# Moving two thirds of a conditioning product from TensorE to VectorE, and loading expert weights in 2 MiB pieces, in a hybrid attention and mixture-of-experts layer

## The reference, cut to what matters

```python
mod = c @ w_ada + b_ada                       # (1, 6144): six vectors of 1024
sh1, sc1, g1, sh2, sc2, g2 = split(mod, 6)
h = rms_norm(x, norm1_g) * (1 + sc1) + sh1    # x: 256 tokens x 1024
proj = h @ w_in                               # 8192 columns
merged = sigmoid(ga) * (diff_attention @ w_pa) + sigmoid(gb) * (stick_breaking @ w_pb)
x = x + g1 * (merged @ w_o)
h = rms_norm(x, norm2_g) * (1 + sc2) + sh2
# top 4 of 32 experts for each token
g, u = split(h_e @ w_gu[e] + b_gu[e], 2)      # w_gu[e]: 1024 x 2048
act = (min(u) + 1) * min(g) * sigmoid(1.702 * min(g))
x = x + g2 * sum(gate * (act @ w_down[e] + b_down[e]))   # w_down[e]: 1024 x 1024
out = rms_norm(x, final_g)
```

## Time and profile before

| | |
|---|---|
| median of 3 runs | 1394.11 us (1392.26 to 1394.58) |
| the profiled execution, its own time | 1394.88 us |
| its span, first to last instruction | 1392.9 us |
| TensorE busy | 1315.2 us, 94% |
| VectorE busy | 434.4 us, 31% |
| ScalarE busy | 186.8 us, 13% |
| moved from and to HBM | 477.54 MB, mean 343 GB/s |

### The profile page before, as it was taken

How to read it: one execution, slowest core, us unless ns; L and a number is a source line. 1 busy time by engine, 2 the same in 40 slices (tenths; PEclk the granted TensorE clock), 3 DMA queues, 4 the chain that set the end, 5 groups by cost and what they waited for, 6 DMA issues and landing times.

```text
span 1392.9 us, 16985 instructions
## 1 busy us (share of the span) xinstructions
PE 1315.2 (94%) x6058; PEld 600.3 (43%) x6059; DVE 434.4 (31%) x911; ACT 186.8 (13%) x378; POOL 15.7 (1%) x48
## 2 busy tenths in 40 slices
PE   4999999999998999999999999999999996999997
PEld 2876775878853333333333323333333331333332
DVE  1000441433124434233423323333332432333333
ACT  3001321343011100010001000001000100001001
POOL 0000000110000000000000000000000000000000
PEclk9999999999997999999999999999999997999999
DMA  9736656333756999999999999999999999499994
GB/s 365 281 121 243 240 193 218 133 122 121 306 239 262 400 422 422 422 421 421 422 422 422 422 422 422 416 422 422 422 423 422 422 422 422 174 423 422 422 422 178
DMA packets 84246, 477.54 MB, mean 343 GB/s; under 512 B 8435, under 2 KB 8764, under 8 KB 31996
## 3 DMA queue, kind: packets, MB, share of 16 engines
q1 hardware_dynamic: 83940, 476.12, 84.2%
q10 hardware_dynamic: 280, 1.05, 0.2%
HBM read 476.09 MB, written 1.05 MB: 343 GB/s over the span
## 4 chain that ended last, share of the span: by engine, by line
PE 84%; DMA 8%; SPq 5%; DVE 1%; ACT 1%; issue 1%; DVEq 0%
PE bank L1437 28%; PE bank L1469 14%; PE bank L1156 12%; DMA down_ring<-in_w_down 6%; PE bank L1389 4%; PE bank L1276 4%; PE bank L1147 4%; PE bank L1426 4%; PE bank L1404 3%; SPq L365 3%; PE bank L1337 2%; DMA gu_ring<-in_w_in 2%; SPq L370 2%; PE bank L1397 1%; ACT scratch L646 1%; PE bank L1101 1%
## 5 line engine op out<-in xcount | busy, mean ns | idle before, releaser
L1437 PE MATMUL bank<-gu_ring,scratch 128*64 128x512 f32 x2048 | 463.7, 600 | 4.9 <-issue 3.7
L1437 PEld LDWEIGHTS bank<-gu_ring,scratch 128*64 128x64 f32 x2048 | 142.5, 138 | 291.6 <-issue 287.7
L1469 PE MATMUL bank<-down_ring,scratch 128*64 128x512 f32 x1024 | 230.3, 597 | 5.8 <-DMA down_ring<-in_w_down 5.7
L1156 PE MATMUL bank<-gu_ring 128*128 128x256 f32 x768 | 173.3, 384 | 2.3 <-DMA gu_ring<-in_w_in 2.3
L1156 PEld LDWEIGHTS bank<-gu_ring 128*128 128x128 f32 x768 | 145.2, 192 | 27.3 <-issue 6.9
L1469 PEld LDWEIGHTS bank<-down_ring,scratch 128*64 128x64 f32 x1024 | 69.2, 137 | 144.0 <-issue 123.8
L650 ACT ACTIVATE scratch<-bank 128x512 f32<-128x512 f32 x32 | 19.1, 597 | 714.1 <-PE bank L1437 714.1
L983 DVE TENSOR_TENSOR scratch<-bank,bgu 128x512 f32<-128x512 f32 x32 | 22.1, 692 | 280.4 <-PE bank L1404 280.4
L965 DVE TENSOR_TENSOR xres<-xres,bank 128x512 f32<-128x512 f32 x132 | 81.8, 682 | 32.4 <-PE bank L1426 32.4
L997 DVE TENSOR_TENSOR scratch<-bank,scratch 128x512 f32<-128x512 f32 x32 | 22.1, 692 | 188.8 <-PE bank L1469 188.8
L1389 PE MATMUL bank<-xn,onehot 128*64 128x512 f32 x264 | 72.7, 631 | 0.8 <-DVE onehot L918 0.8
(11 more groups left out here) (249 smaller groups left out, 751.6 us busy)
## 6 DMA issues: line engine op xcount, KB each, us to landing
gu_ring<-in_w_gu SPq DMA_DIRECT2D x256, 1024.0 KB, 22.0
down_ring<-in_w_down SPq DMA_DIRECT2D x128, 1024.0 KB, 15.7
gu_ring<-in_w_in SPq DMA_DIRECT2D x32, 1024.0 KB, 7.9
gu_ring<-in_w_ada SPq DMA_DIRECT2D x20, 1024.0 KB, 8.9
down_ring<-in_w_ada SPq DMA_DIRECT2D x4, 1024.0 KB, 10.5
gu_ring<-in_w_pa SPq DMA_DIRECT2D x4, 1024.0 KB, 6.2
gu_ring<-in_w_pb SPq DMA_DIRECT2D x4, 1024.0 KB, 6.1
gu_ring<-in_w_o SPq DMA_DIRECT2D x4, 1024.0 KB, 10.0
```

The costliest lines, as they stand in the source:

```text
L1156: last = M(dst[:, b * T:(b + 1) * T], group_chunk(group, kt // 4)[:, kt % 4, cols], hT[:, kt, :], start=kt == 0, stop=kt == KT - 1)
L1437: last = M(bank[f // 2][64 * a:64 * a + 64, :], xT[:, kt % 4, kt // 4, :], gu_ring[:, 8 * half + kt, f * 512:(f + 1) * 512], start=kt == 0 ...
L1469: last = M(bank[7][64 * a:64 * a + 64, :], act_sb[:, kt % 4, kt // 4, :], down_ring[:, kt // 2, (kt % 2) * D + a * 512:(kt % 2) * D + (a + ...
```

## The change

**1. Parts 1 and 2 of `c @ w_ada` go to VectorE.** For each chunk VectorE multiplies 128 x 2048 weights by a per-partition number (the entry of `c` of that row) and adds it to `ada_sum`. TensorE then only sums over the partitions, with ones as stationary operand: `ada_rows(1)` after `differential(4)`, `ada_rows(2)` after the first half block of group 12. VectorE's two chunks of g = 4 and 5 come before the attention, those of g = 6 to 11 after odd steps and the last step. The ring slots of `ada` groups are released by a counter of their own (`ada_read`).

**2. `ada_columns` makes eight matmuls** with two output columns each in place of four with four, for all three parts; for two of the six vectors it reads every second column.

**3. The experts' weights come in pieces of 2 MiB**, 16 KB in each partition in place of 8: for `w_gu` two neighbouring rows, for `w_down` four. TensorE waits for a piece at every second chunk of `w_gu` and every fourth of `w_down`; SP may reload a piece when two, or four, chunks have been used.

In the diff `ada_products` is now VectorE's and `ada_rows` TensorE's.

**4. Everything that meets these rows follows their order.** The gathered tokens (L1397 before) and the router's transposes of x are read at every second column, the results of `w_gu` (L1404 before) and the biases at every fourth; `norm2_g` and two vectors of `b_ada` come by two small loads and two small transposes more at the start.

```diff
+FILL = {group: n for n, group in enumerate(group for group in GROUPS if group[0] != "ada")}
...
-            def load_gu(expert, half, kt):
-                sp.dma_start(gu_ring[:, 8 * half + kt, :],
-                             w_gu[0, bass.ds(expert, 1), kt * P:(kt + 1) * P, :].rearrange("a p n -> p (a n)")
-                             ).then_inc(slot_in[8 * half + kt], 16)
+            def load_gu(expert, half, j):
+                first = 8 * half + 2 * j
+                sp.dma_start(gu_ring[:, first:first + 2, :].rearrange("p r n -> p (r n)"),
+                             w_gu[0, bass.ds(expert, 1), j * 2 * P:(j + 1) * 2 * P, :]
+                             .rearrange("a (p r) n -> p (a r n)", r=2)).then_inc(slot_in[first], 16)
...
+            def load_down(expert, a):
+                sp.dma_start(down_ring[:, 2 * a:2 * a + 2, :].rearrange("p s n -> p (s n)"),
+                             w_down[0, bass.ds(expert, 1), a * 4 * P:(a + 1) * 4 * P, :]
+                             .rearrange("a (p r) n -> p (a r n)", r=4)).then_inc(down_in[a], 16)
...
+                    former = GROUPS[n - 4]
+                    if former[0] == "ada":
+                        sp.wait_ge(ada_read, 2 * (former[1] - 4) + 2)
+                    else:
+                        sp.wait_ge(filled, 2 * FILL[former] + 2)
...
-                for kt in range(KT):
-                    sp.wait_ge(gu_used, item * 8 + (kt - 15))
-                    load_gu(item, half, kt)
+                for j in range(4):
+                    sp.wait_ge(gu_used, item * 8 + (2 * j - 14))
+                    load_gu(item, half, j)
...
+            def ada_products(g):
+                if g == 8:
+                    dve.wait_ge(ada_summed, 1)
+                for h in range(2):
+                    kt, group = 2 * (g % 4) + h, POS["ada", g]
+                    wait_group(dve, group, h)
+                    chunk, c_col = gu_ring[:, group_slots(group)[h], :], vec[:, R_C + kt:R_C + kt + 1]
+                    if kt == 0:
+                        last = V.tensor_scalar(ada_sum, chunk, c_col, None, ALU.mult)
+                    else:
+                        dve.wait_ge(ada_read, 2 * (g - 4) + h)
+                        last = V.scalar_tensor_tensor(ada_sum, chunk, c_col, ada_sum, op0=ALU.mult, op1=ALU.add)
+                    last.then_inc(ada_read, 1)
...
+                if s % 2 == 1 or s == DAH + 2:
+                    ada_products(6 + s // 2)
...
+            def ada_rows(part_):
+                pe.wait_ge(rows_ready, part_)
+                pe.wait_ge(ada_read, 8 * part_)
+                for q in range(4):
+                    last = M(bank[5][32 * q:32 * q + 32, :], ones[:, 0:32], ada_sum[:, q * CW:(q + 1) * CW],
+                             start=True, stop=True, skip_group_check=True)
+                last.then_inc(ada_summed, 1)
...
+            def transposes_by_fours(b, src):
+                for j in range(4):
+                    last = nc.tensor.transpose(bank[b][:, j * P:(j + 1) * P], src[:, j:4 * P:4], ident[:])
+                return last
```

More of the change, by code:

```diff
@@ L204, in build @@
         cols_done = sem("cols_done")
+        ada_read = sem("ada_read")
+        ada_summed = sem("ada_summed")
         sigmoid_ready = sem("sigmoid_ready")
@@ L1081, in _ @@
             nc.tensor.transpose(bank[7][:, 0:R_END], vt, ident[0:R_END, 0:R_END]).then_inc(vecT_done, 1)
+            pe.wait_ge(pairs_in, 32)
+            for r in range(2):
+                last = nc.tensor.transpose(bank[5][:, 12 * r:12 * r + 12], vt_pairs[:, r:2 * P:2], ident[0:12, 0:12])
+            last.then_inc(pairsT_done, 1)
             pe.wait_ge(vec_ready, 2)
@@ L1199, in _ @@
                         differential(s)
-                    if h == 0 and g == 8:
+                    if (g, h) == (8, 0):
+                        ada_rows(1)
+                    if (g, h) == (8, 1):
                         ada_columns(1)
-                if g >= ADA_1:
-                    ada_rows(g)
                 if g == 3:
                     pe.wait_ge(bgu_in, 16)
-                    for a in range(2):
-                        for i in range(2):
-                            last = nc.tensor.transpose(bank[6][:, (2 * a + i) * P:(2 * a + i + 1) * P],
-                                                       bgu_rows[:, a, i:2 * P:2], ident[:])
+                    for n in range(4):
+                        last = nc.tensor.transpose(bank[6][:, n * P:(n + 1) * P], bgu_rows[:, n:4 * P:4], ident[:])
                     last.then_inc(bgu_done, 1)
@@ L1306, in _ @@
                 if s == 0:
-                    ada_columns(ADA_PARTS - 1)
+                    ada_rows(2)
+                if s == 1:
+                    ada_columns(2)
                 if s < SBH + 2:
@@ L1345, in transpose_x1 @@
                 for n in range(4):
+                    first = half * 512 + (n // 2) * 2 * P + n % 2
                     last = nc.tensor.transpose(bank[b + half][:, n * P:(n + 1) * P],
[L1347 removed]
+                                               xres[:, tt, first:first + 2 * P - 1:2], ident[:])
                 last.then_inc(xT_done, 1)
@@ L1392, in take, with transposes_by_pairs @@
                     last.then_inc(taken_done, 1)
-            def transposes(b, src):
-                for j in range(4):
-                    last = nc.tensor.transpose(bank[b][:, j * P:(j + 1) * P], src[:, j * P:(j + 1) * P], ident[:])
-                return last
-            def transposes_by_rows(b, src):
+            def transposes_by_pairs(b, src):
                 for j in range(4):
@@ L1405, in transposes_by_rows @@
                 return last
+            def transposes_by_fours(b, src):
+                for j in range(4):
+                    last = nc.tensor.transpose(bank[b][:, j * P:(j + 1) * P], src[:, j:4 * P:4], ident[:])
+                return last
             def take_transposed(item):
                 pe.wait_ge(xraw_ready, item + 1)
-                transposes(6, x_raw).then_inc(takenT_done, 1)
+                transposes_by_pairs(6, x_raw).then_inc(takenT_done, 1)
             def way_back(item):
@@ L1492, in further @@
                 for c in range(2):
-                    last = nc.tensor.transpose(bank[6][:, c * P:(c + 1) * P], x_raw[:, c * P:(c + 1) * P], ident[:])
+                    last = nc.tensor.transpose(bank[6][:, c * P:(c + 1) * P], x_raw[:, c:2 * P:2], ident[:])
                 last.then_inc(f_takenT, 1)
```

161 lines of the change are left out of this document (83 added, 78 removed).

## The result

The changed kernel takes **1378.26 us** (median of 4 runs, 1375.38 to 1380.52) against 1393.18 of before beside it; the ratio is 0.9887, with a 95% interval from 0.9873 to 0.9901. Measured once more it was 1379.25 us (5 runs), ratio 0.9905 (0.9888 to 0.9923). Over all nine runs its mean is 1379.0, and that of all 56 runs of the kernel before is 1393.6: **-14.7 us** where -12.1 was forecast. The executions of either kernel scatter with a standard deviation of 2 us, and the profiled one of the changed kernel is the fastest of its nine, 1375.38 us, against the profiled 1394.88 of before. So the difference of the two traces, -19.5 us, holds some 5 us of chance, and the text says where.

A forecast was written before the change was run, and what follows sets the result against it. TensorE bounds the first part; in the experts TensorE and full-rate DMA are close, with 9.2 us of waiting. First part -9.6, experts -2.5 (waiting -5.7, strided order +3.2), total -12.1 from 1394.11: 1382 us, range 1378 to 1410.

The forecast's parts named there:

- VectorE's part: First part: TensorE loses product stretches, -14.8 us; with sums, columns, start, attention and router the net is -9.6 us.
- this sign of the prediction: In the attention, VectorE's block before an even step ends before the scores come: 4.58 us against a 4.59 us gap.
- Larger packets: Experts' weight loads: 16 KB packets save 1.6%, 29.34 us an expert in place of 29.82; bounds nothing and 3.3%.
- The stock: Experts' weights loaded ahead: 15.3 us left of 18.8, lasting 13 of 16 experts; three wait 1.17 each, 3.5 us.
- Strided transposes: In the experts: every second column costs +0.10 us an expert, +3.2 in all; every fourth nothing more, with little confidence.
- One reading: Transposes of gathered tokens: a weight load at every second column takes +56 ns, of which the stream shows a fifth.
- The faster transfers behind expert 16: In the experts: waiting for weights ends at expert 16, where the load order changes; no gain counted from there on.
- The clock: Whole kernel: the forecast's sum has no term for TensorE's granted clock.
- A: Rival, experts: every fourth column is dear in L1404's eight loads, 114 ns each; slower, 1408 us; chance 0.33.
- B: Rival, experts: loads at every fourth column cost 20 to 90 ns more; 1391 us, from 1384 to 1401; chance 0.13.
- C: Rival, experts' loads: larger packets give nothing, DMA stays at 29.82 us an expert; 1389.5 us; chance 0.07.
- D: Rival, attention: VectorE becomes the wait, TensorE waits half a block at four steps, 9 us; 1391 us; chance 0.05.

The follow-up runs named there:

- vec_more: Changed kernel with one more VectorE operation over 2048 columns in each block of g = 6 to 10, result unread; 1380.95 us, ratio 0.9901.
- experiment 3: Changed kernel, transposes of the w_gu results at steps 1 and 4, then 8 and 16, in even and odd experts; 27.97, 28.15, 28.09, 28.09 us an expert.
- e1_ada: Kernel before with only the w_ada products moved to VectorE; loads, row order and four column matmuls as before; 1381.05 us, ratio 0.9912.
- warm_before: Kernel before with unread small matmuls in TensorE's waits in the router and the further pass; 1393.6 us, ratio 1.0.
- warm_after: Changed kernel with unread small matmuls in TensorE's waits in the router and the further pass; 1373.67 us, ratio 0.9849.
- experiment 8: Both kernels without the further pass between two experts: 1367.84 us for the kernel before, 1350.37 us for the changed one.
- e2_pieces: Kernel before with only the 2 MiB pieces, the new row order and eight column matmuls; TensorE keeps the w_ada products; 1394.12 us, ratio 1.0006.
- e3_small: Changed kernel with each 2 MiB piece issued as two 1 MiB transfers, 8 KB in a partition, same row order; 1385.03 us, ratio 0.9943.
- best_pos: Like warm_after, with four matmuls for part 0's columns and 4 unread matmuls at the start; 1373.74 us, ratio 0.9849.
- best: Like warm_after, with four matmuls for part 0's columns and 28 unread matmuls at the start; 1376.16 us, ratio 0.9867.

## What the prediction had right, and the step that failed

**VectorE's part: right.** TensorE lost 14.8 us and got the sums over partitions, +1.98 (forecast +1.85), the columns of two parts, 1.75 (1.8), a later start, +1.14 (0.7, bounds 0 and 1.4), nothing at the end of the attention (0.5) and +0.75 in the router (0.4): 9.2 us in place of 9.6. Alone, part 1 measured -12.9 against 12.8 from its rows. The part of the start is mostly low clock: the eight matmuls of part 0's columns took 3.11 us, two thirds of it at 1.2 GHz, the eight of a later part 1.75 us at 2.4 GHz. The blocks took 4.80 us and not 4.58, since the multiply-add takes 2.35 us and not 2.29. So a block ended no earlier than the scores came (VectorE has no idle time before L774 at 145.38), and this sign of the prediction did not come true; TensorE did not wait all the same, and `vec_more` shows how much room was left.

**Larger packets: right in kind, lucky in size.** Where weights bound it, an expert took 29.37 us in both traces of the changed kernel, forecast 29.34. But the forecast was the middle between two bounds with no row of its own. The stock lasted 13 experts, as forecast; the waiting was 2.6 us in the first trace, 3.4 in the second (29.15, 29.38 and 29.36), against 3.5.

**Strided transposes: right, with little to go by.** L1443 costs 0.09 us an expert (0.10), L1449 nothing. The choice rested on one row with a wide step, on another engine; experiment 3 now has it on TensorE. One reading was off: of the 56 ns that a load takes longer the stream shows 22 (0.09 us for four), two fifths and not a fifth. No sum used it.

**The faster transfers behind expert 16: the step that failed.** The prediction says of the waiting: "It ends at expert 16, where the load order changes." So it priced the faster transfers at nothing from there on. The new order does give new stock there, but the pass uses it up, because it wants expert 25's `w_down` a turn early. In the trace of before its last piece was issued at 1148.0 and took 23.5 us to land:

```profile
L370 SPq DMA_DIRECT2D down_ring<-in_w_down x1: 333/333/333, 1148.0 to 1148.0; - x1
...
DMA to landing us min/median/max: 23.5/23.5/23.5
```

That is 1171.6, or 272.9 us behind g16. TensorE's products with it ran from 1168.06 to 1174.3, so slowly (granted clock 0.62 from 1166 to 1175) that no wait shows. In the changed kernel the last piece (issued at 1131.5, 20.6 us to landing) lands 270.8 us behind g16, 2.1 earlier. `e1_ada`, with the old pieces and less low clock there, does come upon the transfers: TensorE waits 0.7 us for `w_gu` and 0.2 for `w_down` in its pass.

```profile
1135.22 23.59 DMA down_ring<-in_w_down
1158.85 1.11 PE bank L1542 x8
```

What the left-out term is worth shows where the clock is held: 2.1 us net of 0.7 for the order between `warm_before` and `warm_after`, so some 2.8 in place of nothing. Without the pass it is 5.6 us of waiting behind g16 (experiment 8).

How much of it the plain change collected is not shown. From g16 to the give behind the pass it takes 286.9 us in place of 289.9, but that holds the clock too. The distance of the two gives around the pass is 61.7 and 61.9 us in the two traces of the changed kernel, 64.1 in `vec_more`, which has the same loads and three stretches of low clock there in place of two; it is 65.3 before, 63.4 in `e1_ada` and 64.0 in `e2_pieces`. So the clock moves the pass by as much as the transfers do. These distances also don't explain why the whole brought 2.6 us more than its parts: in the pass the two parts save 1.9 and 1.3, together nearly the whole's 3.5. That the forecast was 2.6 us short fits a term of this size, but this last step is argued, and the sum of the parts being equal to the forecast may be chance.

**The clock: also priced at nothing.** By the mean over all runs it took no side between the kernels (granted clock 0.984 and 0.985). Within one kernel a mean clock lower by 0.001 went with 0.5 us more in the kernel before and 1.0 in the changed one. In the two profiled executions it made 5 to 6 of the 19.5 us: 2.6 in the first expert and most of the rest in the pass (L1512's 6.22 us against L1559's 3.64).

The rivals: A is refuted by loads of 209 ns; B falls with it; C by 428 GB/s and `e3_small`; D by `vec_more`.

## What to carry to other kernels

Where transfers and an engine run at nearly one rate, follow the stock through the whole span and look at each place where it is used up early: there the chain may show a slow engine while a transfer stands right behind it. Work out an edit's gain at each such place, not only where waits show. And before reading a difference of two traces as an effect, look at the granted clock behind each longer wait of TensorE: here the executions of one kernel differed by 5 us.

## What was not expected of the hardware

- A weight load of 128 x 128 fp32 takes 140 ns from consecutive columns and 195 to 210 from every 2nd, 4th, 8th or 16th.
- The loop's first product came 1.4 us behind the instruction ahead of it in `warm_after` and `best_pos`, waiting for VectorE, and 4.0 to 4.1 us in `best` and `warm_before`, waiting for nothing that the profile shows. With as many instructions ahead of the loop as in `warm_after` the wait was short again; that it hangs on the loop's place in the program is so far only argued, from one pair.
- Unread matmuls in waits kept the mean granted clock at 0.992 to 0.995, against 0.984 to 0.985 without. They brought 5 us in the changed kernel and none in the one before, whose loop entered late and whose pass then waited 2.9 us for transfers. The runs still spread by 0.6, 1.5, 2.5, 5.1 and 6.6 us in the five kernels that have them.
